# A two-block transformer kernel on one core: the second block's activations kept as a split pair, and its projections reordered

## The reference

```python
h = rms_norm(x, g_mix[l])
proj = h @ w_in[l]                       # (512, 1024) @ (1024, 4352)
sb_q, sb_k, sb_v, d_q, d_k, d_v, m_q = jnp.split(proj, IN_SPLITS, axis=-1)
y_sb  = stick_breaking_attention(sb_q, sb_k, sb_v)      # 8 heads of 64
y_dil = dilated_mixture(d_q, d_k, d_v, g_q_dil, g_k_dil) # 12 heads of 64, strides 1, 4, 16
y_mem = memory_attention(m_q, rms_norm(mem, g_mem), w_mem_kv, g_q_mem, g_k_mem) # 4 heads of 128
gates = jax.nn.sigmoid(h @ w_gate[l] + b_gate[l])
merged = gates[0] * (y_sb @ w_o_sb) + gates[1] * (y_dil @ w_o_dil) + gates[2] * (y_mem @ w_o_mem)
x = x + merged @ w_out[l]
x = x + peer_ffn(rms_norm(x, g_ffn[l]), ...)
```

## Time and profile before

| | us |
|---|---|
| runs | 3095.22, 3091.81, 3093.50; median 3093.50 |
| span of the profiled execution, first to last instruction | 3091.8 |
| PE busy | 2926.7 |
| DVE busy | 2016.5 |
| ACT busy | 1316.6 |
| first products, PE | 1014.5 to 1060.9 |
| stick stage | 1061.9 to 1315.3 |
| memory stage up to its step 10 | 1315.3 to 1398.6 |

### The profile page before, as it was taken

How to read it: one execution, slowest core, us unless ns; L and a number is a source line. 1 busy time by engine, 2 the same in 40 slices (tenths; PEclk the granted TensorE clock), 3 DMA queues, 4 the chain that set the end, 5 groups by cost and what they waited for, 6 DMA issues and landing times. The chain is left out here.

```text
span 3091.8 us, 36029 instructions
## 1 busy us (share of the span) xinstructions
PE 2926.7 (95%) x13679; PEld 2349.3 (76%) x13679; DVE 2016.5 (65%) x3259; ACT 1316.6 (43%) x2119; POOL 408.6 (13%) x293
## 2 busy tenths in 40 slices
PE   7999999799997998989899899999999989999999
PEld 5756787688885655747566678999999988788777
DVE  4574433588887246525422268889898858888886
ACT  4334422477776223425222143336667643232322
POOL 0000000010011000000000000021112324544442
PEclk9999999799998998999799999999999999999999
DMA  4120062467766110210022132477777979999996
GB/s 165 44 65 19 24 182 106 182 265 283 298 256 238 68 55 28 82 56 21 1 94 101 50 142 96 150 246 246 271 283 287 341 301 347 385 390 383 385 383 260
DMA packets 159467, 585.94 MB, mean 190 GB/s; under 512 B 15168, under 2 KB 86464, under 8 KB 131008
## 3 DMA queue, kind: packets, MB, share of 16 engines
q1 hardware_dynamic: 100544, 421.59, 37.2%
q0 software_dynamic: 41472, 138.45, 12.0%
q10 hardware_dynamic: 17280, 23.60, 2.1%
HBM read 556.81 MB, written 64.52 MB: 201 GB/s over the span
## 5 line engine op out<-in xcount | busy, mean ns | idle before, releaser
L2183 POOL DMA_INDIRECT RG<-in_un,EI x128 | 178.8, 1397 | 1434.8 <-DVE EI L2435 1020.1
L2550 PE MATMUL bank<-VH,GL 128*128 128x512 f32 x768 | 302.7, 394 | 7.4 <-DVE VR1r L2261 3.0
L2552 PE MATMUL bank<-VH,GH 128*128 128x512 f32 x768 | 300.6, 391 | 0.0
L2183 POOL DMA_INDIRECT RG<-in_vn,EI x128 | 184.8, 1444 | 260.9 <-DVE X L2197 232.2
L2197 DVE SCALAR_TENSOR_TENSOR X<-RG,DG,X 128x1024 f32<-128x1024 f32 x128 | 164.2, 1283 | 47.1 <-DMA RG<-in_vn,EI 43.3
L2194 DVE CUSTOM_DVE_ANT_0 RG<-RG,HR 128x1024 f32<-128x1024 f32 x128 | 156.4, 1222 | 40.0 <-DMA RG<-in_un,EI 39.2
L2550 PEld LDWEIGHTS bank<-VH,GL 128*128 128x128 f32 x768 | 144.2, 188 | 44.5 <-issue 10.2
L2167 PE MATMUL bank<-HTl,UH1r 128*128 128x384 f32 x512 | 172.7, 337 | 0.0
L2168 PE MATMUL bank<-HTh,UH1r 128*128 128x384 f32 x512 | 172.5, 337 | 0.0
L2168 PE MATMUL bank<-HTh,UH0r 128*128 128x384 f32 x512 | 172.2, 336 | 0.0
L2167 PE MATMUL bank<-HTl,UH0r 128*128 128x384 f32 x512 | 172.0, 336 | 0.0
(11 more groups left out here) (618 smaller groups left out, 7522.2 us busy)
## 6 DMA issues: line engine op xcount, KB each, us to landing
UR<-in_u SPq DMA_DIRECT2D x64, 1024.0 KB, 6.7
VR<-in_vn SPq DMA_DIRECT2D x32, 2048.0 KB, 9.5
UP<-in_wup SPq DMA_DIRECT2D x22, 2048.0 KB, 7.8
DN<-in_wdn SPq DMA_DIRECT2D x32, 1024.0 KB, 7.2
W<-in_weights SPq DMA_DIRECT2D x20, 1536.0 KB, 7.1
W<-in_weights SPq DMA_DIRECT2D x14, 2048.0 KB, 8.4
wspill<-VR SPq DMA_DIRECT2D x12, 2048.0 KB, 8.8
aspill<-GA ACTq DMA_DIRECT2D x120, 192.0 KB, 5.3
```

The source lines that it names most:

```text
L2183: e.indirect_dma_start(RG[q % RR], None, d["un" if what == "u" else "vn"][:, :], off).then_inc(*row_in[q % RR].up(16))
L2550: e.matmul(bk, r(gl[:, a, t]), r(vh[:, a, :]), start=g == 0 and a == 0, stop=False)
L2552: i = e.matmul(bk, r(gh[:, a, t]), r(vh[:, a, :]), start=False, stop=g == 31 and a == 3)
```

## The change

The normalized activations of the second block are kept as the pair `HTh`, `HTl`, and `HT` isn't written. `HTh` lies in the memory of `X`, so x is stored to DRAM (`xs`) after the first products' norms and loaded again at the end of the gates. Stick v and memory q are made behind stick q and k, in three passes, and memory q goes to DRAM (`mqs`) and is loaded in the memory stage. The dilated projections are made in three passes. Their weights are split part by part inside the steps of the stick stage: in each step s below 24 with s mod 4 equal to 2 or 3, `act_job` stands last in `act_jobs` and `dve_job` last in `dve_jobs`. The gates need no split of the activations.

```diff
@@ first products
-            norm2 = Norm(c0, "mix2", None, 2, HT, "mix2", rows=rows2)
+            norm2 = Norm(c0, "mix2", None, 2, None, "mix2", rows=rows2)
+            def act_job(e, t, part):
+                if part == 0:
+                    wait_weight(e, t)
+                    if t >= 26:
+                        e.wait_ge(*j_mm(4 * (t - 26) + 4))
+                c = span(part, sizes[t] // 2)
+                e.activation(r(JW[t % 2][1][:, c]), JW[t % 2][0][:, c], ACT.Copy).then_inc(*jw_hi.up(1))
+
+            def dve_job(e, t, part):
+                c = span(part, sizes[t] // 2)
+                e.wait_ge(*jw_hi(2 * (t - 24) + part + 1))
+                e.tensor_tensor(r(JW[t % 2][2][:, c]), JW[t % 2][0][:, c], JW[t % 2][1][:, c], ALU.subtract).then_inc(*jw_lo.up(1))
...
-                    e.activation(r(h2h[:, k, :]), bank[k], ACT.Copy, scale=norm2.gain[:, k:k + 1]).then_inc(*h2_hi.up(1))
-                    if k % 2:
-                        e.wait_ge(*h2_lo(k))
-                        e.activation(HT[:, k - 1, :], bank[k - 1], ACT.Copy, scale=norm2.gain[:, k - 1:k]).then_inc(*n_keptA.up(1))
-                act_second(e, 22)
+                    e.activation(r(HTh[:, k, :]), bank[k], ACT.Copy, scale=norm2.gain[:, k:k + 1]).then_inc(*h2_hi.up(1))
+                act_second(e, 1)
...
-                norm2.wait(e)
...
+                for u in range(8, 16):
+                    g, tb = divmod(u, 4)
+                    e.wait_ge(*qw_lo(2 * g + 2))
+                    e.wait_ge(*(q_keptV if u % 2 else q_keptA)((u - 8) // 2 + 1))
+                    hi, lo = SECOND[g][1:]
+                    for k in range(8):
+                        c = span(k, 512)
+                        e.matmul(bank[u - 8], r(HTl[:, k, span(tb)]), r(hi[:, c]), start=k == 0, stop=False)
+                        e.matmul(bank[u - 8], r(HTh[:, k, span(tb)]), r(lo[:, c]), start=False, stop=False)
+                        i = e.matmul(bank[u - 8], r(HTh[:, k, span(tb)]), r(hi[:, c]), start=False, stop=k == 7)
+                    i.then_inc(*q_mm.up(1))
...
+                    e.wait_ge(*f_fin(4))
+                    e.dma_start(d["xs"].rearrange("(b p) n -> p b n", p=128), XN[:, :, 0:1024]).then_inc(*xs_done.up(16))
+                    e.wait_ge(*xs_done(16))
+                    e.dma_start(WM, w_src(MQ)).then_inc(*m_in.up(16))
...
+                    for tb in range(4):
+                        e.wait_ge(*(q_keptV if tb % 2 else q_keptA)(7 + tb // 2))
+                        e.dma_start(d["mqs"][span(tb), :], stage[:, tb, :]).then_inc(*mq_done.up(16))
+                    e.wait_ge(*mq_done(64))
@@ stick stage
-                    if u < 4:
-                        return 23, 512, lambda k: ht(k, u)
-                    if u < 20:
-                        return 24 + (u - 4) // 4, 384, lambda k: ht(k, u % 4)
+                    if u < 16:
+                        return 24 + u // 4, 384, lambda x, k: x[:, k, span(u % 4)]
...
                         for k in range(8):
-                            i = e.matmul(bank[4 + u % 2][:, 0:w], lhs(k), weight(t)[:, span(k, w)], start=k == 0, stop=k == 7)
+                            if u % 4 == 0 and k % 4 == 0:
+                                e.wait_ge(*jw_lo(2 * (t - 24) + k // 4 + 1))
+                            c = span(k, w)
+                            e.matmul(bk, r(lhs(xl, k)), r(hi[:, c]), start=k == 0, stop=False)
+                            e.matmul(bk, r(lhs(xh, k)), r(lo[:, c]), start=False, stop=False)
+                            i = e.matmul(bk, r(lhs(xh, k)), r(hi[:, c]), start=False, stop=k == 7)
...
                         e.activation(dst, bank[4 + u % 2][:, 0:w], ACT.Copy).then_inc(*j_out.up(1))
+                    if step < 24 and step % 4 >= 2:
+                        act_job(e, 25 + step // 4, step % 2)
...
+                        for x, o in ((HTh, HPh), (HTl, HPl)):
+                            src = x.rearrange("p k (l b r) -> p b k r l", b=4, r=4)[:, b]
+                            i = e.tensor_copy(r(o.rearrange("p k (r l) -> p k r l", r=4)), src)
+                        i.then_inc(*j_cols.up(1))
...
+                    if step < 24 and step % 4 >= 2:
+                        dve_job(e, 25 + step // 4, step % 2)
@@ memory stage
-                JOB0, ATT0 = 2, 16
+                TURN, JOB0, NORM0, ATT0 = 3, 4, 2, 10
...
+                        e.dma_start(BD, d["bd"]).then_inc(*bd_in.up(16))
                         e.dma_start(ME, d["mem"].rearrange("(b p) n -> p b n", p=128)).then_inc(*me_in.up(16))
-                        e.dma_start(BD, d["bd"]).then_inc(*bd_in.up(16))
+                        for tb in range(4):
+                            e.dma_start(MS[tb], d["mqs"][span(tb), :]).then_inc(*mq_in[tb].up(16))
...
-                            if 10 <= step < ATT0:
-
-                                if step == 10:
-                                    e.wait_ge(*k_out(7))
-                                warm(e, 1, 4)
@@ gates
-                        for k in range(8):
-                            e.wait_ge(*self.h_hi(k + 1))
-                            e.tensor_tensor(r(HTl[:, k, :]), HT[:, k, :], self.HTh[:, k, :], ALU.subtract).then_inc(*self.h_lo.up(1))
...
+                        e.wait_ge(*g2.gated(24))
+                        e.dma_start(X, d["xs"].rearrange("(b p) n -> p b n", p=128)).then_inc(*in_x.up(16))
```

More of the change, by code:

```diff
@@ L1545, in _ @@
                     act_two_norms(e)
-                    for u in range(0, 8, 2):
+                    for u in range(0, 16, 2):
+                        if u == 4:
+                            act_second(e, 3)
+                        if u == 14:
+                            for part in range(2):
+                                act_job(e, 24, part)
                         e.wait_ge(*q_mm(u + 1))
-                        e.activation((qT, kT)[u // 4][:, u % 4, :], bank[u], ACT.Copy, scale=(0.125, 1.0)[u // 4]).then_inc(*q_keptA.up(1))
+                        dst, scale = second_out(u)
+                        e.activation(dst, bank[u % 8], ACT.Copy, scale=scale).then_inc(*q_keptA.up(1))
                 @block.vector
@@ L1580, in _ @@
                     dve_two_norms(e)
-                    for u in range(1, 8, 2):
+                    for u in range(1, 16, 2):
+                        if u == 5:
+                            dve_second(e, 3)
+                        if u == 15:
+                            for part in range(2):
+                                dve_job(e, 24, part)
                         e.wait_ge(*q_mm(u + 1))
-                        e.tensor_scalar((qT, kT)[u // 4][:, u % 4, :], bank[u], (0.125, 1.0)[u // 4], None, ALU.mult).then_inc(*q_keptV.up(1))
+                        dst, scale = second_out(u)
+                        e.tensor_scalar(dst, bank[u % 8], scale, None, ALU.mult).then_inc(*q_keptV.up(1))
         release()
@@ L1834, in dve_jobs @@
+                        i.then_inc(*j_cols.up(1))
+                    n = step - 3
+                    if 0 <= n < 16:
                         e.wait_ge(*j_root(n + 1))
@@ L1844, in _ @@
                     def _(e):
-                        load_weights(e, 34)
+                        for t in range(26, 31):
+                            load_job(e, t)
+                        load_weights(e, 33)
                     @block.tensor
@@ L1934, in pe_memory @@
                                 i.then_inc(*k_turn.up(1))
-                    u = step - JOB0
-                    if 0 <= u < 8:
-                        t = 31 if u < 4 else 32 if u < 6 else 33
+                    p = step - JOB0
+                    if 0 <= p < 4:
+                        t = 31 + p // 2
                         wait_weight(e, t)
+                        if p == 0:
+                            e.wait_ge(*k_kept(4))
+                        if p >= 2:
+                            e.wait_ge(*k_out(p - 1))
+                        for k in range(8):
+                            i = e.matmul(bank[4 + p % 2], MT[:, k, span(p % 2)], weight(t)[:, span(k, 512)], start=k == 0, stop=k == 7)
+                        i.then_inc(*k_mm.up(1))
+                    u = step - NORM0 - 2
+                    if 0 <= u < 6:
+                        e.wait_ge(*k_norm(u + 1))
                         if u == 0:
                             e.wait_ge(*k_kept(4))
-                        if u >= 2:
-                            e.wait_ge(*k_out(u - 1))
-                        for k in range(8):
-                            lhs = ht(k, u) if u < 4 else MT[:, k, span(u % 2)]
-                            i = e.matmul(bank[4 + u % 2], lhs, weight(t)[:, span(k, 512)], start=k == 0, stop=k == 7)
-                        i.then_inc(*k_mm.up(1))
-                    u = step - JOB0 - 4
-                    if 0 <= u < 6:
-                        e.wait_ge(*k_norm(u + 1))
                         if u >= 2:
```

246 lines of the change are left out of this document (130 added, 116 removed).

## The result

The changed kernel takes 3134.0 us (median of 4 runs, 3133.95 to 3135.66), the kernel before 3092.7 (4 runs). The ratio is 1.0133, with a 95% interval of 1.0119 to 1.0148, so the change costs 41 us. The forecast was 3143 us, with 3108 to 3172 as its range.

What follows compares the result with a forecast made beforehand. PE, busy 2926.7 of 3091.8 us, was taken as the bound. First products +38.9, stick work −28.0, waits +45, clock +16, memory stage −22, gates −0.7 gave +49: span 3141, median 3143 us, range 3108 to 3172.

Steps and rivals of the forecast that it cites:

- first products: Stage ahead of the stick stage: earlier start gives back 7.8 us, eight more units cost 44.3, store wait 2.4; together +38.9.
- stick stage: Stage with the dilated projections: PE's work −28, waits +45, lower clock +16, so 253.4 becomes 286 us.
- memory stage: Four plain units leave −28.4, their steps give back +10, busy-keeping matmuls −5.3, light steps' clock +1.5; −22, bounds −15 and −28.
- gates, all behind them: At the gates PE no longer waits for the low part of `HT`, −0.7 us; loading x again costs nothing.
- The new waits: Stick stage: PE waits for DVE's late mask ahead of scores in eight steps, 39 us; +45 in all, bounds 0 and 55.
- The clock: Stick stage: jobs behind the eight waits run at a lower clock, 2 us each, +16; bounds 0 and 33.
- the rival in which the clock stays down: Lower clock holds through the stick stage's waits: clock term 33 us and more, time 3160 to 3175; chance 0.14.
- Half-sized waits: Stick stage waits are there at half size: +22 for waits, +8 for clock, 3112 to 3120 us; chance 0.13.
- PE's own work in the stick stage: Stick v leaves −29.9, four jobless steps +15.6, three-pass units −17.8 and −5.8, strided units +7.9, column copy +2.0; −28.0.
- The strided loads: Stick stage, four dilated v units reading every fourth column: weight loads set the pace, 5.93 us each, +7.9; otherwise 2.83 each.
- The six matmuls that kept PE busy: Memory stage: these fillers leave and save 0.89 us each, −5.3.
- the split is hidden: Stick stage: ACT and DVE find room for the split, waits and clock terms fall away; −12, 3082 us, chance 0.12.

## Why the prediction was right, and where its sizes were off

The profiled span grew from 3091.8 to 3133.8 us, by 42.0, where the sum said 49. By stages:

| step | predicted | measured |
|---|---|---|
| first products | +38.9 | +40.1 |
| stick stage | +33 (286 us) | +13.4 (266.8 us) |
| memory stage | −22 | −11.8 |
| gates, all behind them | −0.7 | +2.1 |
| all ahead of the first products | 0 | −1.7 |

**First products: right.** PE's first product was to come at 1008.5 and came at 1008.12. The stage was to end near 1100, and ended at 1100.34. At its end PE idles for 3.22 us, 1.05 before, so the store of memory q costs 2.2 where 2.4 were assumed.

**The new waits: the mechanism is shown, the size a fifth too large.** The split stands behind a copy that PE's last transposes release, and in front of the mask that PE needs next. The forecast put a wait behind eight named steps, and the profile has it in each of them. Two kernels that only move the copy (in the changed kernel and in the kernel before) take the loss away. PE's idle time ahead of transposes and scores in the eight steps adds up to 41.3 us, and in the kernel with the copy at the head to 9.2. So the waits cost 32 us there, and 3.7 more in step 4, which makes 36 instead of 45. The forecast named the scores as the place. Over half of the wait, 18 of the 32 us, lies earlier, in front of the transposes. `PTs` is copied by DVE in steps 7, 11 and 19 (L1789), behind the difference, and by ACT in the even steps (L1762), behind the weight copy. The forecast had neither. In the mean a step loses 4 us, near the lower end of the 4.1 to 6.3 given for one step: part of what the sum counted on top was idle time that these steps have in any case (the 9.2).

**The clock: about right.** The changed kernel's stage is 49.8 us longer than with the copy at the head, and 36 of it is idle time. The other 14 us are the clock: up to step 30 PE's work itself takes 17 us more in the changed kernel, most of it in the jobs behind the waits, and in the last ten steps 3.4 less, since there it is the kernel with the copy at the head that runs slowly. In step 7 the job's matmuls start every 0.32 us up to 1157.5 and every 0.17 from then on; it takes 6.55 us where step 6 has 4.28. The term was 16. In the rival in which the clock stays down it was 33 and more: the granted clock is 0.84 over the stage, and the jobs recover before their end, so that rival falls. Half-sized waits fall as well, by 36 against 22.

**PE's own work in the stick stage: too small a gain.** It was put at −28.0. The kernel with the copy at the head, in which hardly any wait is left, shows 217.0 less 253.4, −36.4. The 8.4 us between them are 5.7 + 5.4 − 2.7. First, the sum adds 3.9 us for each of four steps at the end without a job, as if they were new. They stood in the stage before, with their stick part beside a job (step 28 took 5.76 us, 3.56 of them its job). Outside the jobs' matmuls the stage grows by 10.5 us (85.7 to 96.2), where the sum had 16.2. Second, the kernel before had six jobs (steps 15, 16, 18, 20, 22 and 24) that took 11.1 us more than their neighbours of the same form, one of them that of the earlier trace rows. The kernel with the copy at the head has three, with 5.7 us. The estimate had left the clock of the kernel before as it was. Against that, all jobs at the full rate fall by 41.5 us and not by the 44.2 of the sum.

**The strided loads: right.** Predicted 5.93 us a unit, measured 5.65, and not the 2.83 that a packed unit would take. The trace shows a load every 0.235 us, and one every 0.117 in the packed units, which are issued in the same form. By the Trainium skill (TensorE: Matmul & The Clock Gate, LDWEIGHTS (loading the stationary operand)) a load of 128 columns would take 107 ns, and no stride is named there. The measurement decides against that here, where the columns lie 16 bytes apart.

**The memory stage: the step that failed.** "The six matmuls that kept PE busy leave at 0.89 each, −5.3." From the stage's start to PE's scores of its step 9 (1399.54 before, 1431.37 now) it fell by 20.0 us, close to the −18.4 of four plain units less what their steps give back. Behind that the sum had −3.8, and the trace has +8.2. With the fillers gone PE runs its next dense stretch, 24.5 us, at 0.51 of the full clock. The six steps from there on take 23.2 us, and 12.7 in all three profiles of kernels with two fillers in each of steps 8 and 9. These 10.4 us are most of the 12.0 by which sum and trace differ. In whole times the fillers give 4.6 to 6.5 us. They had been priced as work that is saved, without asking what the clock does when they go. All this is measured on the kernel with the split at the head; on the changed kernel itself fillers weren't tried. The rest, under 2 us, stays open, and single profiles of one kernel differ by 7 us in this stage (181.4 and 188.3). Not six but ten such matmuls left: four stood in step 0 of the stage, in PE's wait for the memory rows. PE idled 6.99 us ahead of them before and idles 12.36 us at the start of the stage now. Its scores of step 1 came 14.4 us after that start before and come after 12.9 now, so these four show no cost.

**The sum.** The stick stage came out 19.6 us below the forecast (waits 9, own work 8, clock 2) and the memory stage 10.2 above it. That 42 is so near to 49 is in part luck: these errors have opposite signs. The 2.1 us at the gates and behind and the 1.7 ahead of the first products belong to no step; single executions differ by as much.

**The rival "the split is hidden"** was given 3082 us. The kernel with the copy at the head measured 3079.0 and 3082.2. The rival fails for the change as it was made, and its price holds for the kernel with the call at the other end of a list. That it holds so closely is luck of the same kind, since that kernel too has the larger gain in the stick stage and the slow stretch in the memory stage.

## What to carry to other kernels

In a loop where each engine works through its own list, an added operation costs what its place makes it cost. Find the wait that it stands behind and the consumer that stands behind it. An operation that needs nothing from the current step goes ahead of the step's late wait. Here the last place made 50 us of eight splits of some 3 us each, and the first place next to nothing.

Matmuls that only keep PE busy are not work to be struck off. Before they are removed, look at the granted clock of the dense stretch behind them, and afterwards look again.

## What the runs showed of the hardware that had not been expected

- A long dense stretch can run slowly from its start. In the changed kernel PE was busy for 8.5 of the 10 us ahead of it (first row), at a granted clock of 0.98, and then for 24.5 us without a pause at 0.51. With four fillers, in the kernel that has the split at the head, it was busy for all of the 10 us at the same place (second row), and the clock stayed at 1.00: 123 matmuls in 20 us, against 66 at 0.52.

```profile
1421.00:1431.00 10.00, 8.49 (x41) 5.18 (x40) 3.59 (x13) 4.44 (x13) 0.00 (x0) 0.98 0.45 157
1371.00:1381.00 10.00, 10.00 (x40) 5.41 (x39) 3.65 (x13) 4.79 (x14) 0.00 (x0) 1.00 0.42 157
```

- Where PE had idled for over 4 us, six filler parts took 4.31 us, 0.72 each, and the job behind them ran at the full rate. What the fillers took beyond the wait and what the steps behind gave back came to the same.
- A load of 128 float32 columns that lie 16 bytes apart starts every 0.235 us in a stream of three-pass matmuls of 256 columns. In the packed units of the changed kernel a matmul starts every 0.118 us.
- The scatter differs from kernel to kernel. The one with the split at the head ran from 3073.4 to 3091.8 us in 12 runs on one chip, the kernel before from 3087.5 to 3098.2 in 17, the changed kernel from 3134.0 to 3135.7 in 4. In the first of these it goes with the mean granted clock: 0.963 to 0.964 in the three runs under 3077 us, 0.957 to 0.959 in the four over 3087.
